# State update of a decode step with 32-row products in four row groups, and the sample transposes moved one chunk up

## The reference

```
C_new[b] = decay[b] * C[b] + sum over its 4 tokens s of  ws[b,s] * v[b,s] (outer) k[b,s]     # 256 x 256
```

## Time and profile before

| what | value |
|---|---|
| time, median of 3 runs | 1494.39 us (1492.83 to 1494.52) |
| the profiled execution, its own time | 1494.43 us |
| its span, first to last instruction | 1492.9 us |
| busy PE / PEld | 99% / 97% |
| busy DVE / ACT / POOL | 59% / 42% / 12% |
| mean granted TensorE clock | 0.995 of full |
| DMA | 289.62 MB, mean 194 GB/s |

### The profile page before, as it was taken

How to read it: one execution, slowest core, us unless ns; L and a number is a source line. 1 busy time by engine, 2 the same in 40 slices (tenths; PEclk the granted TensorE clock), 3 DMA queues, 4 the chain that set the end, 5 groups by cost and what they waited for, 6 DMA issues and landing times. The chain is left out here.

```text
span 1492.9 us, 31290 instructions
## 1 busy us (share of the span) xinstructions
PE 1472.3 (99%) x11147; PEld 1452.5 (97%) x11147; DVE 888.1 (59%) x1481; ACT 626.3 (42%) x885; POOL 184.8 (12%) x331
## 2 busy tenths in 40 slices
PE   9999999999999999999999999999999999999996
PEld 9999999999999999999999999999999999999996
DVE  7756565554434438676767676777767554445444
ACT  6433343333333334444544454545354433333452
POOL 4000000001000000303030303031312000000000
PEclk9999999999999999999999999999999999999998
DMA  7764655556555576595959596969697666555543
GB/s 234 211 163 139 180 149 174 164 164 221 184 172 176 175 199 184 151 289 158 300 149 294 154 294 166 279 170 276 173 278 174 200 182 177 172 175 191 172 156 141
DMA packets 310006, 289.62 MB, mean 194 GB/s; under 512 B 82728, under 2 KB 297456, under 8 KB 309168
## 3 DMA queue, kind: packets, MB, share of 16 engines
q1 hardware_dynamic: 291424, 243.05, 58.3%
q0 software_dynamic: 18288, 45.97, 9.0%
q10 hardware_dynamic: 256, 0.10, 0.0%
HBM read 263.62 MB, written 25.42 MB: 194 GB/s over the span
## 5 line engine op out<-in xcount | busy, mean ns | idle before, releaser
L1086 DVE TENSOR_TENSOR wlo<-raw,whi 128x1024 fp32r<-128x1024 f32 x416 | 507.2, 1222 | 528.4 <-ACT whi L818 527.4
L444 PE MATMUL ps<-xh,whi 128*128 128x288 f32 x2560 | 763.1, 298 | 0.0
L818 ACT ACTIVATE whi<-raw 128x1024 fp32r<-128x1024 f32 x416 | 440.5, 1060 | 754.4 <-PE ps L446 730.3
L446 PE MATMUL ps<-xh,wlo 128*128 128x288 f32 x2560 | 756.7, 296 | 0.0
L445 PE MATMUL ps<-xl,whi 128*128 128x288 f32 x2560 | 755.8, 295 | 0.0
L444 PEld LDWEIGHTS ps<-xh,whi 128*128 128x128 f32 x2560 | 482.2, 188 | 6.9 <-issue 6.2
L446 PEld LDWEIGHTS ps<-xh,wlo 128*128 128x128 f32 x2560 | 481.5, 188 | 0.0
L445 PEld LDWEIGHTS ps<-xl,whi 128*128 128x128 f32 x2560 | 481.2, 188 | 0.2
L445 PE MATMUL ps<-yl,whi 128*128 128x288 f32 x512 | 151.6, 296 | 0.0
L444 PE MATMUL ps<-yh,whi 128*128 128x288 f32 x512 | 150.8, 295 | 0.0
L446 PE MATMUL ps<-yh,wlo 128*128 128x288 f32 x512 | 150.7, 294 | 0.0
(11 more groups left out here) (354 smaller groups left out, 1094.1 us busy)
## 6 DMA issues: line engine op xcount, KB each, us to landing
raw<-in_w_in_dram SPq DMA_DIRECT2D x320, 512.0 KB, 4.0
raw<-in_w_pb_dram SPq DMA_DIRECT2D x32, 512.0 KB, 3.5
Cin<-in_state_mlstm_C_dram POOLq DMA_DIRECT2D x16, 1024.0 KB, 8.7
Xb<-in_state_mlstm_C_dram SPq DMA_DIRECT2D x256, 64.0 KB, 3.7
out_dram<-Cin POOLq DMA_DIRECT2D x16, 1024.0 KB, 6.3
raw<-in_w_pa_dram SPq DMA_DIRECT2D x32, 512.0 KB, 3.5
raw<-in_w_out_dram SPq DMA_DIRECT2D x32, 512.0 KB, 3.6
part_d<-part POOLq DMA_DIRECT2D x8, 288.0 KB, 3.1
```

What stands on the lines that cost most here:

```text
L444: nc.tensor.matmul(out, whi[:, c, kk, cols], mh_[:, k, :], start=(k == 0), stop=False)
L446: last = nc.tensor.matmul(out, wlo[:, c, kk, cols], mh_[:, k, :], start=False, stop=(k == KT - 1))
L818: nc.scalar.activation(whi[:, c], raw[:, c], ACT.Copy).then_inc(hi_ready, 1)
L1086: nc.vector.tensor_tensor(wlo[:, c], raw[:, c], whi[:, c].bitcast(F32), ALU.subtract).then_inc(lo_ready, 1)
```

## The change

Each sequence now has its own group of 32 rows. `kv4` is laid out so that rows 32g to 32g+31 hold the tokens of sequences 2g and 2g+1, each repeated four times; a repeated copy has one of three roles (high x high, high x low, low x high; the fourth is zero), set by the new constants `v_sign`, `v_low` and `k_low`. ScalarE writes `vm` directly, one version for even and one for odd sequences, and `vst` and the masking by `of_sequence` go. A product reads 32 rows: `vm[rows, b % 2]` and `kst[rows]`. The order of the sequences is 0, 2, 4, 6, 1, 3, 5, 7, in three visits of four, three and one sequences, in the order value half 0 of all, then value half 1 of all. The first visit uses banks 6, 7, 2, 3, the others 2, 3, 5 and 2. The transposes of k and of the samples stand one chunk earlier, with the ScalarE copies behind them; the state additions, the product of the weights and the update of n change places on VectorE; the wait for `part_free` goes from VectorE to ScalarE; `load_c` and the stores take every second sequence.

Cut to the parts that carry work or waits (`...` where lines are left out):

```diff
+STATE_ORDER = (0, 2, 4, 6, 1, 3, 5, 7)
+STATE_BANK = (6, 7, 2, 3, 2, 3, 5, 2)
+STATE_VISITS = ((0, 4), (4, 7), (7, 8))
...
@@ tensor
-        def new_state(h, b):
-
-            pe.wait_ge(vm_set, 8 * h + b + 1)
-            if b >= 3:
-                pe.wait_ge(cs_ev, 8 * h + b - 2)
+        def new_states(h, visit):
+
+            first, end = STATE_VISITS[visit]
+            if visit:
+                pe.wait_ge(cs_ev, 8 * h + 3 + visit)
             for vh in range(2):
-                last = nc.tensor.matmul(ps[:, NEW_BANK[b % 3], DH * vh:DH * vh + DH],
-                                        vm[:, b % 4, vh::2], kst[:], start=True, stop=True)
+                for n in range(first, end):
+                    b = STATE_ORDER[n]
+                    rows = rows_of(b // 2)
+                    last = nc.tensor.matmul(ps[:, STATE_BANK[n], DH * vh:DH * vh + DH], vm[rows, b % 2, vh::2],
+                                            kst[rows, :], start=True, stop=True)
             last.then_inc(cs_mm, 1)
...
-                if c == 2:
+                if c == 1:
                     pe.wait_ge(p_set, h + 1)
...
-                if c == 3:
+                if c == 2:
                     pe.wait_ge(kt_ev, h + 1)
                     pe.wait_ge(kv4_set, 2 * h + 2)
...
                     pe.wait_ge(slot_free[1], H_USE[1] + 2 + 2 * h)
-                    for b in range(2):
-                        new_state(h, b)
+                    new_states(h, 0)
                 if c == 1:

                     pe.wait_ge(tiles_set, h + 1)
                     pe.wait_ge(vt_ev, h + 1)
+                    pe.wait_ge(cs_ev, 8 * h + 2)
...
-                    for b in range(2, 4):
-                        new_state(h, b)
                 if c == 2:
-                    for b in range(4, 6):
-                        new_state(h, b)
+                    new_states(h, 1)
...
                     last.then_inc(ht_t, 1)
-                    for b in range(6, NB):
-                        new_state(h, b)
-
-                    pe.wait_ge(cs_ev, 8 * h + 6)
+                    new_states(h, 2)
+
+                    pe.wait_ge(cs_ev, 8 * h + 7)
@@ scalar, loop of pair o
-                if c == 3:
+                if c == 2:
                     act.wait_ge(kvs_t, h + 1)
                     nc.scalar.activation(kst[:], ps[:, 5, 0:DH], ACT.Identity, scale=gq[:, 2, ds(h + 64, 1)])
-                    nc.scalar.activation(vst[:], ps[:, 5, DH:2 * DH], ACT.Copy)
-                    nc.scalar.activation(ktok[0:S, 2, :], ps[0:S, 5, 0:DH], ACT.Identity,
-                                         scale=gq[0:S, 2, ds(h + 64, 1)])
-                    nc.scalar.activation(vtok_h[0:S, 2, 0:DH], ps[0:S, 5, DH:2 * DH],
-                                         ACT.Copy).then_inc(kvs_ev, 1)
+                    for par in range(2):
+                        nc.scalar.activation(vm[:, par, :], ps[:, 5, DH:2 * DH], ACT.Identity,
+                                             scale=v_sign[:, par:par + 1])
+                    nc.scalar.activation(vtok_h[:, 2, 0:DH], ps[:, 5, DH:2 * DH], ACT.Copy).then_inc(kvs_ev, 1)
...
+                    act.wait_ge(part_free, 9)
                     act.wait_ge(inter_mm, 2 * h + 2)
@@ vector, ahead of the heads
-        dve.wait_ge(part_free, 9)
...
+        nc.vector.tensor_tensor(v_sign[:], role[:, :, 1], role[:, :, 2], ALU.add)
+        nc.vector.tensor_scalar(v_low[:], role[:, :, 2], -1.0, None, ALU.mult)
+        role_s(nc.vector.tensor_tensor(r3[:, 0:1], mask8[:, 1:2], mask8[:, 5:6], ALU.add))
+        nc.vector.tensor_tensor(v_sign[:], v_sign[:], role[:, :, 0], ALU.subtract)
+        role_s(nc.vector.tensor_scalar(k_low[:], gq[:, 2, 64:64 + HEADS], r3[:, 0:1], None, ALU.mult))
@@ vector, loop of pair o (the copies to kv4 and the n update move as well)
                 if c == 3:
+                    dve.wait_ge(kvs_ev, h + 1)
+                    nc.vector.scalar_tensor_tensor(kst[:], ps[:, 5, 0:DH], k_low[:, ds(h, 1)], kst[:].bitcast(F32),
+                                                   ALU.mult, ALU.subtract)
+                    for par in range(2):
+                        last = nc.vector.scalar_tensor_tensor(vm[:, par, :], ps[:, 5, DH:2 * DH], v_low[:, par:par + 1],
+                                                              vm[:, par, :].bitcast(F32), ALU.mult, ALU.add)
+                    last.then_inc(st_lo, 1)
+                split_lo(H0 + 4 + 5 * h, c)
...
@@ vector, loop of pair za
                 split_lo(H0 + 5 + 5 * h, c)
                 if c == 0:
                     add_state(h, 0)
-                    of_sequence(h, 4)
                     add_state(h, 1)
-                    of_sequence(h, 5)
...
-                if c == 2:
-                    add_state(h, 4)
-                    add_state(h, 5)
+                if c == 3:
+                    for n in range(4, 7):
+                        add_state(h, n)
...
-            for b in range(6, NB):
-                add_state(h, b)
+            add_state(h, 7)
```

More of the change, by code:

```diff
@@ L128, in build @@
     mask8 = fixed("mask8", [P, NB])
+    v_sign = fixed("v_sign", [P, 2])
+    v_low = fixed("v_low", [P, 2])
+    k_low = fixed("k_low", [P, HEADS])
     eye8 = fixed("eye8", [P, HEADS])
@@ L220, in build @@
     kst = a("kst", [P, DH], F32R)
-    vst = a("vst", [P, DH], F32R)
     W = a("W", [P, 512])
@@ L1381, in turn_blocks, with add_state @@
             nc.vector.transpose(of_c(b).rearrange("p k (j s) -> p j k s", s=32), Xb[:, b]).then_inc(block_turned, 1)
[L1383 to L1392, removed]
+        def add_state(h, n):
+            if n % 4 == 0:
+                dve.wait_ge(c_in[n // 4], 16 * h + 16)
+            visit = [first <= n < end for first, end in STATE_VISITS].index(True)
+            dve.wait_ge(cs_mm, len(STATE_VISITS) * h + visit + 1)
+            b = STATE_ORDER[n]
             nc.vector.scalar_tensor_tensor(Cin[:, b], Cin[:, b], dec_bc[:, ds(8 * h + b, 1)],
-                                           ps[:, NEW_BANK[b % 3], :].rearrange("p (v k) -> p v k", v=2),
+                                           ps[:, STATE_BANK[n], :].rearrange("p (v k) -> p v k", v=2),
                                            ALU.mult, ALU.add).then_inc(cs_ev, 1)
@@ L1448, in _ @@
                     add_n(h, 0)
+                if c == 3:
+                    dve.wait_ge(silu_k, 3 * h + 3)
+                    for j in range(2):
+                        last = nc.vector.tensor_copy(
+                            kv4[:, 0, j].rearrange("p (b r t) -> p b r t", r=4, t=TS),
+                            bc(qk[:, 2 + j, TP:T].rearrange("p (b t) -> p b t", t=TS), 2, [P, NB, 4, TS]))
+                    last.then_inc(kv4_set, 1)
                 split_lo(H0 + 3 + 5 * h, c)
@@ L1465, in _ @@
                                         cn[:].rearrange("p j r -> p (j r)")).then_inc(cst_ev, 1)
-                if c == 3:
-                    dve.wait_ge(silu_k, 3 * h + 3)
-                    nc.vector.tensor_copy(kv4[:, 0].rearrange("p j (n s) -> p j n s", s=S),
-                                          bc(qk[:, 2:4, TP:T], 2, [P, 2, P // S, S])).then_inc(kv4_set, 1)
+            for c in range(CHUNKS):
+                if c == 0:
+                    turn_blocks(h, 4)
+                    turn_blocks(h, 5)
+                if c == 1:
+                    turn_blocks(h, 6)
+                    turn_blocks(h, 7)
+                    add_n(h, 1)
+                if c == 1:
+                    dve.wait_ge(v_ev, h + 1)
+                    for j in range(2):
+                        last = nc.vector.tensor_copy(
+                            kv4[:, 1, j].rearrange("p (b r t) -> p b r t", r=4, t=TS),
+                            bc(vz[:, j, TP:T].rearrange("p (b t) -> p b t", t=TS), 2, [P, NB, 4, TS]))
+                    last.then_inc(kv4_set, 1)
+                if c == 3:
+                    dve.wait_ge(kvs_ev, h + 1)
[6 more added lines that the diff above has]
+                split_lo(H0 + 4 + 5 * h, c)
+                if c == 0:
+                    dve.wait_ge(s_mm, h + 1)
+                    dve.wait_ge(w_exp, h + 1)
+                    nc.vector.scalar_tensor_tensor(W[:, 0:416], ps[:, 5, 0:416], DH ** -0.5, W[:, 0:416],
+                                                   ALU.mult, ALU.mult).then_inc(p_set, 1)
+                if c == 2:
                     dve.wait_ge(wsb_set, h + 1)
@@ L1484, in _ @@
             for c in range(CHUNKS):
[L1485 to L1494, removed]
-                    nc.vector.tensor_copy(kv4[:, 1].rearrange("p j (n s) -> p j n s", s=S),
-                                          bc(vz[:, :, TP:T], 2, [P, 2, P // S, S])).then_inc(kv4_set, 1)
-                if c == 0:
-                    dve.wait_ge(s_mm, h + 1)
-                    dve.wait_ge(w_exp, h + 1)
-                    nc.vector.scalar_tensor_tensor(W[:, 0:384], ps[:, 5, 0:384], DH ** -0.5, W[:, 0:384],
```

(17 more changed lines are left out.)

30 lines of the change are left out of this document (17 added, 13 removed).

## The result

The changed kernel takes 1531.12 us (median of 4 runs, 1530.7 to 1532.28), the kernel before 1494.45 (4 runs, 1492.83 to 1495.14): ratio 1.0248, 95% interval 1.023 to 1.0266. It is slower by 36.7 us; forecast were 31 us more and 1526 us. The profiled execution has a span of 1528.4 us, 35.5 more than before.

The account below looks back on a forecast made before the run. TensorE, busy 1472.3 of 1492.9 us, was taken as the bound. Eight heads of -0.52 + 0.38 + 3.56 give 27.4, less 4.0 once, plus 8 for the clock: +31, so 1526 us, own range 1521 to 1532.

Parts of the forecast that it names:

- parts 1 and 2: After chunk 0 of a head's last pair: sample transposes one chunk earlier, overlapping 32-row state products; -0.52 us a head.
- E0: The time at which chunk 0 of the last pair of a head, za, ends; 614.43 us in the kernel before.
- part 3: Second visit, after chunk 1 of the last pair: it waits for the fourth state addition; +0.38 us a head.
- E1: The time at which chunk 1 of the last pair of a head, za, ends; 619.23 us in the kernel before.
- part 4: End of the head: additions behind the split for chunk 3 make TensorE wait twice; +3.56 us a head.
- E3: The time at which chunk 3 of the last pair of a head, za, ends; 628.71 us in the kernel before.
- part 5: Ahead of the heads: with part_free awaited on ScalarE, the bcrow wait and low clock behind it go; -4.0 us once.
- part 6: Clock falls to 1.2 GHz around the end-of-head waits in 7 of 8 heads; +8 us, between 0 and 12.
- Rival (a): The end-of-head waits come, but the clock stays at 2.4 GHz; 1518 us, chance 0.20.
- the prediction's signs: Trace observations that would show it right, among them eight waits of 0.6 us at the second visit.
- Rival (c): At the end of the head, additions 4 to 6 don't hold TensorE; faster, 1489 us, chance 0.07.
- the 8 x 3.05 for a free overlap: Eight heads' cost with free row-group overlap and no clock loss, giving 1515 us near the 8-in-10 range's lower end.

Follow-up runs that it names:

- fill: The changed kernel with extra identity products, 11 ahead of the last visit and 3 ahead of C_p's products, filling TensorE's waits; 1517.51 us.
- adds_c2: The changed kernel with state additions n = 4, 5, 6 behind the split for chunk 2 instead of chunk 3; 1491.07 us.
- before_adds_c3: The kernel before with its additions 4 and 5 moved behind the split for chunk 3 instead of chunk 2; 1524.94 us.
- only_n4: The changed kernel with only addition n = 4 moved behind the split for chunk 2; 1528.55 us, runs from 1518.72 to 1533.14.
- adds_early: As adds_c2, with additions n = 2, 3 also moved directly behind n = 0, 1, after the split for chunk 0; 1487.06 us.

## Why the prediction was right, and where its sizes were off

All terms in us; measured are those of the changed kernel's trace against the one before, and for the clock the medians of fill. With the profiled 12.4 for the clock the sum is +35.3, and the profiled spans differ by 35.5.

| step | predicted | measured |
|---|---|---|
| parts 1 and 2, behind E0, a head | -0.52 | 1.08 - 1.61 = -0.53 |
| part 3, E1 to the start of chunk 3, a head | +0.38 | 621.88 - 0.13 - 615.37 = 6.38, before 6.30: +0.08 |
| part 4, E3 to C_p's products, a head | +3.56 | 4.60 - 1.14 = +3.46 |
| C_p's products to the next chunk, clock aside | 0 | 1.65 - 1.54 = +0.11 |
| eight heads of these | +27.4 | 8 x 3.12 = +25.0 |
| part 5, once | -4.0 | -4.1 (from the first matmul of the heads to E3: 77.84 before, 73.32 after, less -0.45 of the rows above); -2.9 to -4.3 alone |
| part 6, clock | +8 | +13.6 (fill, medians; 12.4 between the profiled spans) |
| pitch of yh, yl, mh, ml | none | +2.0 |
| sum | +31 | 25.0 - 4.1 + 13.6 + 2.0 = +36.5; runs 36.7 |

**Part 4 was right in kind and size.** It was read from the code (one buffer for both pairs, so the split waits for the chunk) and priced with the earlier trace rows; adds_c2 takes the waits away, before_adds_c3 makes them without the rest of the change. The two waits of about 2.7 and 0.8 us forecast were 2.47 and 0.69 us in the first head. The 0.10 us too much a head is the handoff: I took up to 0.14 us from the end of an addition to TensorE's start, and it is 0.05.

**Part 6 is the mis-sized term.** I took 7 heads of 8 and 1.15 us each. Six of eight show it between L730 and the next chunk (2.05 us or more), but in the first head 1.2 GHz lasted 6.8 us, twice the stretch behind the wait for bcrow that I had measured it by. fp32 products of C_p, eight records, fall in it. The time at 1.2 GHz behind a wait isn't a constant to be carried from one place to another, and only_n4 shows that it changes between runs of one kernel. The term's own upper bound, 12 us, was passed. That the time still lies inside the forecast's own 1521 to 1532, by 1 us, is in part luck: part 3 (2.4 us too much) and part 4 (0.8) made up for some of it. Rival (a), with the clock kept, is what fill makes: 1518 us worked out, 1517.5 measured, and that closeness is luck too, since its 27.4 stands for 25.0 and the 2.0 that I did not know of.

**Part 3 was overpriced.** I took 0.70 us for the visit of 6 and 5.98 for its start; they are 0.55 us from its first product (621.20 to 621.88 - 0.13) and 5.83. of_sequence, which I gave nothing for, stood ahead of the fourth addition by little after all: it starts at E1 + 5.03, before at 5.11. The wait at the second visit is 0.32 to 0.34 us, where the prediction's signs had 0.6.

**Parts 1 and 2 came out by the sum.** The visit of 8 is 0.65 us (1.08 less 0.43 for four transposes), I took 0.70 with 0.39. The four row groups overlap: four products start within 0.01 us, and the same eight as full products would be 0.94. What the trace couldn't give is now in it: 8 products cost 0.65 us, 6 products the same 0.65 (adds_early, 620.82 + 0.13 to 621.73 - 0.13), and 2 products of one group still 0.53 (adds_early, 625.44 to 625.97). So a visit costs nearly the same however many products it has; the third visit, for one sequence, takes 0.53 us where the kernel before took 0.56 for two sequences. That the sum of parts 1 and 2 came out to 0.01 us is helped by small errors against each other: the transposes take 0.43 us and not 0.39, the visit 0.65 and not 0.70. The Trainium skill's rule that tiles load and multiply in parallel ("TensorEngine Tiling (Array Packing)", Key Properties) holds for row groups here as well, with 0.65 us for the eight beside 0.94.

**Rival (c)** is what adds_c2 is: 1489 us worked out for additions that are done in time, 1491.07 measured, 1489 without the address term. **Missing altogether** were the pitch of the streamed tiles (+2.0 us) and the 0.11 us a head from C_p's products to the next chunk (0.9 us). One bound can't be followed: the 8 x 3.05 for a free overlap. With both visits at 0.24 us the prediction's own figures give 3.42 - 0.92 = 2.50 us a head, so 1510 us and not 1515; nothing else rests on it.

## What to carry to other kernels

When small steps are placed by hand between the parts of a pipeline with a fixed number of buffers, ask for each what it stands *behind*: a step behind the split for chunk c can't begin before TensorE has finished chunk c of the pair before, whatever its own inputs are. A long wait on the bounding engine can cost more than its length: behind those of 2.3 to 2.7 us the clock fell in most heads, while the kernels with only the waits of 0.3 or 0.5 us kept it. If such a wait can't be removed, idle products in it took over a third of the whole cost away here (13.6 of 36.7 us). And few, full visits to the tiled form pay: two products cost 0.53 us, eight cost 0.65.

## What the runs showed of the hardware that I had not expected

- Three constants that take 96 bytes in all moved the streamed tiles, and the matmuls reading them (fp32r, 288 columns) went from 132.2 to 132.8 ns apart to 133.3; 32 bytes of padding brought them to 132.2 (mh, ml) and 132.6 to 132.7 (yh, yl). Why not all the way for yh stays open, and so does why before_adds_c3 differs from the kernel before at the same address.
- Four row groups overlap with weights of 128 columns (four products start within 0.01 to 0.02 us, the second of a group 0.23 us after its first), and it made no difference (0.65 us both ways) whether neighbours in the order used the same group.
- The granted clock fell to 1.2 GHz behind most of the waits of 2.3 to 2.7 us, which had some transposes ahead of them and two products behind or ahead; how long it stayed there differed by head (L730 to the next chunk 1.65 to 3.23 us) and by run (1518.7 to 1533.1 us for one kernel).
